# Seven block products in place of eight in the down projections of four convolution stages

## The chip, the cores and the metric

The kernel runs on one core of a Trainium2 chip. The metric is the device time of one execution in microseconds; of several runs the median is taken. TensorE is the engine that multiplies matrices (PE in the profile, with PEld for its weight loads), VectorE (DVE) does elementwise sums, ScalarE (ACT) the functions, GpSimd (POOL) and SyncE (SP) issue transfers.

## What is computed

The reference is a transformer in float32 with a sequence of 256 tokens and a width of 1024: two layers of a first kind, then four layers of a second kind. Each of the four ends with a gated feed-forward part with a short convolution:

```python
def conv_glu_ffn(h, up_w, conv_w, conv_b, down_w):
    gate, up = jnp.split(h @ up_w, 2, axis=-1)
    gate = causal_dwconv(gate, conv_w) + conv_b
    return (jax.nn.silu(gate) * up) @ down_w
...
        x = x + conv_glu_ffn(rmsnorm_2(x, ln_ffn[i]), f_up[i], f_conv_w[i], f_conv_b[i],
                             f_down[i]).astype(x.dtype)
```

The hidden width is 2816, which is 22 row blocks of 128. The change bears on the last product, the down projection: 256 tokens x 2816 times 2816 x 1024, added onto x. After the fourth layer a last RMS norm gives the output.

## The kernel before, in words

Everything is float32. The weights come as 244 chunks of 128 x 4096 (2 MB each) through `ring`, a buffer of four chunks: `chunk_load` on SyncE (line 2665) loads chunk c when TensorE has counted `chunks_used` up to c - 3, that is when chunk c - 4 has been used; `arrived` is an engine's wait for a chunk. The chunks are used strictly in order.

A convolution stage (`convglu_pe`, `convglu_act`, `convglu_dve`) goes through eleven chunks of the up projection. For chunk j TensorE computes 256 gate channels into one PSUM bank and 256 up channels into the next (banks 4 and 5 for even j, 6 and 7 for odd j; `channels_pe`, line 468). ScalarE copies the gate bank to `cbuf` (line 2343), VectorE does three taps of the convolution into `aT` (lines 2356 and 2362), ScalarE the SiLU (line 2347), and VectorE multiplies with the up bank (line 2367). That makes two of the 22 row blocks of `aT`, which is channels x tokens. VectorE counts `convglu_dve_done` four times a chunk, ScalarE `convglu_act_done` twice a chunk.

The down projection (`down_pe` with nk=22; in the last stage `last_pe`) takes six chunks with four row blocks each. For chunks 0 to 3 (16 row blocks; line 341, in the last stage line 1083) TensorE does, for each row block, two token tiles x two halves of the 1024 columns, into banks 0 to 3, bank 2t + half. A matmul is 128 x 128 weights against 128 x 512 moving data and becomes two TensorE instructions. The tail, chunks 4 and 5 with six row blocks (line 360, in the last stage 1095), is done first for token tile 0 and then for tile 1. Ahead of chunk 5 TensorE waits that the last up chunk's product is in `aT` (the `then` wait). When tile 0 is complete, VectorE adds banks 0 and 1 onto `x[:, 0]` (line 445; last stage 1114), ScalarE squares (line 402), VectorE takes the reciprocal and scales (453, 456), and TensorE transposes the scaled tile (line 390) between the chunks 4 and 5 of tile 1. Tile 1 follows in the same way, into the next stage. In the last stage the norm goes to the output instead (lines 1114, 1117, 1120, and the store 1131).

The order on each engine is written out by hand, and each engine's queue runs in that order: on VectorE `convglu_dve` is followed by `down_dve` (or `last_dve`). The four stages that the diff touches are those whose down projections are numbered 8, 11 and 14, and the last one; the other `down_pe` calls with nk=22 (after SwiGLU stages) are left as they are.

Of the kernel before, what the change touches and what calls it, by code (L numbers as in the profile page):

```python
# [6 lines left out]
P = 128  # L7
SEQ = 256
TT = SEQ // P
D = 1024  # L10
# [44 lines left out]
def build(nc, x_in, mem_in, weights_in, ada_in, b_gate_in, w_small1_in, w_small2_in, col_in, row_in, final_norm_in, rope_in, out):  # L55
    with ExitStack() as ctx:
# [4 lines left out]
        def sem(name):  # L61
            return ctx.enter_context(nc.semaphore(name))
# [63 lines left out]
        convglu_dve_done = sem("convglu_dve_done")  # L126
        hgrn_act_done = sem("hgrn_act_done")
# [196 lines left out]
        def down_pe(pe, i, before, c0, nk, ada=(), kc0=None, ki=0, late=None, then=None):  # L324
# [10 lines left out]
            for j in range(nc - 2):  # L335

                w = arrived(pe, c0 + j).rearrange("p (k c) -> p k c", k=4)
                for k in range(4):
                    for t in range(TT):
                        for half in range(2):  # L340
                            last = pe.matmul(ps[:, 2 * t + half, :], aT[:, 4 * j + k, t * P:(t + 1) * P],  # L341
                                             w[:, k, half * 512:(half + 1) * 512], start=(4 * j + k == 0), stop=False)
                last.then_inc(chunks_used, 1)
                if j < len(ada):
                    ada_reduce_pe(pe, ada[j], 6 + ada[j] % 2)
                if late and j == 0:
                    turn(pe, n, 3)
# [4 lines left out]
            for t in range(TT):  # L352
                for c in range(nc - 2, nc):
                    if then and (t, c) == (0, nc - 1):
                        pe.wait_ge(*then)
                    w = arrived(pe, c0 + c) if t == 0 else ring[:, (c0 + c) % R, :]
                    w = w.rearrange("p (k c) -> p k c", k=4)
                    for k in range(min(4, nk - 4 * c)):
                        for half in range(2):
                            last = pe.matmul(ps[:, 2 * t + half, :], aT[:, 4 * c + k, t * P:(t + 1) * P],  # L360
                                             w[:, k, half * 512:(half + 1) * 512], start=(4 * c + k == 0), stop=(4 * c + k == nk - 1))
                    if t == 1:
                        last.then_inc(chunks_used, 1)
# [56 lines left out]
        def down_dve(dve, i, before, c0, nk, gain, shift, gate=None, gi=0, ada=(), mg_col=None):  # L420
# [13 lines left out]
            if ada:  # L434
                ada_take_dve(dve, ada[-1], 6 + ada[-1] % 2)
                dve.wait_ge(ada_taken, ada[-1] + 1)

# [670 lines left out]
        def last_dve(dve):  # L1108

            dve.wait_ge(last_norm_loaded, 16)  # L1110
# [1257 lines left out]

        def hgrn_part(start, half):

            return view(big, start + 1024 * half, 4, SEQ)
# [346 lines left out]
        def _(pe):  # L2718
# [18 lines left out]
            down_pe(pe, 8, (convglu_dve_done, 40), c0=121, nk=22, then=(convglu_dve_done, 44))  # L2737
# [6 lines left out]
            down_pe(pe, 11, (convglu_dve_done, 84), c0=156, nk=22, then=(convglu_dve_done, 88))  # L2744
# [5 lines left out]
            down_pe(pe, 14, (convglu_dve_done, 128), c0=197, nk=22, then=(convglu_dve_done, 132))  # L2750
# [5 lines left out]
            last_pe(pe, (convglu_dve_done, 172), c0=238, then=(convglu_dve_done, 176))  # L2756
# [42 lines left out]
        def _(dve):  # L2799
# [18 lines left out]
            down_dve(dve, 8, (convglu_dve_done, 44), c0=121, nk=22, gain=column('ln_mix_2', 8, KT), shift=zeros)  # L2818
# [5 lines left out]
            down_dve(dve, 11, (convglu_dve_done, 88), c0=156, nk=22, gain=column('ln_mix_2', 16, KT), shift=zeros)  # L2824
# [5 lines left out]
            down_dve(dve, 14, (convglu_dve_done, 132), c0=197, nk=22, gain=column('ln_mix_2', 24, KT), shift=zeros)  # L2830
# [5 lines left out]
            last_dve(dve)  # L2836
# [109 lines left out]
```

## Time and profile before

| | us |
|---|---|
| median of three runs | 3842.44 (3839.93 to 3847.46) |
| profiled execution, whole | 3835.18 |
| its span, first to last instruction | 3833.5 |
| PE busy in the span | 3769.7 (98%) |
| DVE busy | 1064.5 (28%) |
| ACT busy | 722.6 (19%) |
| mean granted TensorE clock | 0.993 of full speed |

The profile is that of one execution. In its rows a PE matmul instruction has a duration of its own, but instructions are pipelined: the spacing from start to start is what adds up, and it is read from the busy time of an unbroken group divided by its count. "Idle before" is an engine's idle time ahead of an instruction, with what ended it. The chain that ended last is followed back from the last instruction, so its pieces are the work and waits that set the end.

### The profile page before, as it was taken

To read this page: it belongs to the slowest core of one execution; us is meant where nothing else is said; L and a number is where in the kernel's file an instruction comes from. 1 tells how busy PE (TensorE), PEld (TensorE's weight loads), DVE (VectorE), ACT (ScalarE), POOL (GpSimd) and SP (SyncE) were. 2 spreads that over 40 slices of the span, in tenths; PEclk is the share of its full clock that TensorE was granted. 3 is DMA by queue.
4 is the path that set the end of the run, shared out by engine and by line. 5 is a ranking of instruction groups with operands and counts; after the bars stand their busy time and mean duration, and the time that the engine had idled before them with its cause. 6 is when DMAs were issued, how large, how long until landed. Compare 5 with 4: busy or idle time off the path is not lost.

```text
span 3833.5 us, 37694 instructions
## 1 busy us (share of the span) xinstructions
PE 3769.7 (98%) x16628; PEld 2706.8 (71%) x16628; DVE 1064.5 (28%) x2082; ACT 722.6 (19%) x1370; POOL 16.2 (0%) x43
## 2 busy tenths in 40 slices
PE   6999999999999999999999999999999999999999
PEld 5856686784678587578766668677666967757784
DVE  5434342410520044102122112136411212431121
ACT  1003300100520053111011211033211103421110
POOL 1000000000000000000000000000000000000000
PEclk8999999999999999999999999999999999999999
DMA  9753486643334433334442434433233344333342
GB/s 376 287 192 133 175 307 230 248 159 148 132 123 154 154 132 110 132 132 154 153 154 88 152 114 154 154 132 110 89 133 129 142 151 149 110 132 132 140 151 99
DMA packets 42450, 598.43 MB, mean 156 GB/s; under 512 B 4736, under 2 KB 4752, under 8 KB 6192
## 3 DMA queue, kind: packets, MB, share of 16 engines
q1 hardware_dynamic: 41024, 589.94, 41.6%
q0 software_dynamic: 1264, 6.10, 0.4%
q8 instruction: 131, 2.15, 0.2%
q14 instruction: 31, 0.25, 0.0%
HBM read 594.97 MB, written 1.05 MB: 155 GB/s over the span
## 4 chain that ended last, share of the span: by engine, by line
PE 95%; DVE 3%; issue 1%; ACT 1%; DMA 0%; DVEq 0%
PE ps L468 37%; PE ps L341 12%; PE ps L360 9%; PE ps L1927 4%; PE ps L380 3%; PE ps L2268 3%; PE ps L1960 3%; PE ps L1435 2%; PE ps L1455 2%; PE ps L664 1%; PE ps L2486 1%; PE ps L1430 1%; PE ps L493 1%; PE ps L1083 1%; PE ps L390 1%
## 5 line engine op out<-in xcount | busy, mean ns | idle before, releaser
L468 PE MATMUL ps<-hT,ring 128*128 128x256 f32 (+1 forms) x7872 | 1438.3, 345 | 3.6 <-DVE stat L322 3.6
L468 PEld LDWEIGHTS ps<-hT,ring 128*128 128x128 f32 x7872 | 1291.8, 191 | 147.3 <-issue 7.7
L341 PE MATMUL ps<-ring,aT 128*128 128x512 f32 x1088 | 471.6, 594 | 0.0
L341 PEld LDWEIGHTS ps<-ring,aT 128*128 128x128 f32 x1088 | 206.7, 191 | 254.5 <-issue 254.1
L360 PE MATMUL ps<-ring,aT 128*128 128x512 f32 x784 | 341.1, 592 | 0.0
L360 PEld LDWEIGHTS ps<-ring,aT 128*128 128x128 f32 x784 | 147.9, 190 | 179.1 <-issue 178.9
L221 DVE SCALAR_TENSOR_TENSOR memT<-big,silu_c,memT 128x512 f32<-128x512 f32 x238 | 179.0, 752 | 8.5
L1927 PE MATMUL ps<-hT,ring 128*128 128x256 f32 x768 | 173.6, 382 | 0.0
L402 ACT ACTIVATE big<-x 128x1024 f32<-128x1024 f32 x34 | 35.9, 1057 | 729.6 <-DVE x L445 409.2
L1927 PEld LDWEIGHTS ps<-hT,ring 128*128 128x128 f32 x768 | 145.7, 192 | 26.2 <-issue 7.7
L2356 DVE TENSOR_SCALAR aT<-cbuf,col 128x256 f32<-128x256 f32 x88 | 27.1, 351 | 415.6 <-ACT cbuf L2343 415.6
L1180 DVE TENSOR_TENSOR aT<-cbuf,ps 128x512 f32<-128x512 f32 x44 | 30.2, 687 | 397.7 <-ACT cbuf L1164 397.7
L1164 ACT ACTIVATE cbuf<-ps 128x512 f32<-128x512 f32 x44 | 26.3, 597 | 578.5 <-PE ps L468 578.5
L445 DVE TENSOR_TENSOR x<-x,ps 128x1024 f32<-128x1024 f32 x22 | 26.9, 1221 | 357.6 <-PE ps L360 349.8
L1960 PE MATMUL ps<-ring,hT 128*128 128x512 f32 x256 | 113.4, 594 | 0.0
L2268 PE MATMUL ps<-ring,big 128*128 128x512 f32 x256 | 112.5, 592 | 0.0
L380 PE MATMUL ps<-big,ring 128*128 128x256 f32 x512 | 111.8, 379 | 0.0
L2089 DVE SCALAR_TENSOR_TENSOR big<-cbuf,col,big 128x256 f32<-128x256 f32 x192 | 80.3, 480 | 105.0 <-ACT big L1976 103.9
L380 PEld LDWEIGHTS ps<-big,ring 128*128 128x128 f32 x512 | 97.0, 190 | 14.7 <-issue 1.9
L2343 ACT COPY cbuf<-ps 128x512 f32<-128x512 f32 x44 | 25.7, 585 | 416.7 <-PE ps L468 416.7
L664 PE MATMUL ps<-hT,ring 128*128 128x256 f32 x448 | 101.3, 385 | 0.0
L664 PEld LDWEIGHTS ps<-hT,ring 128*128 128x128 f32 x448 | 85.4, 193 | 13.2 <-issue 1.9
(474 smaller groups left out, 3211.3 us busy)
## 6 DMA issues: line engine op xcount, KB each, us to landing
ring<-weights_in SPq DMA_DIRECT2D x244, 2048.0 KB, 7.7
big<-ada_in SPq DMA_DIRECT2D x34, 2048.0 KB, 7.7
ring<-ada_in SPq DMA_DIRECT2D x2, 2048.0 KB, 27.3
big<-b_gate_in POOLq DMA_DIRECT2D x1, 1536.0 KB, 15.1
x<-x_in SPq DMA_DIRECT2D x1, 1024.0 KB, 4.9
big<-b_gate_in POOLq DMA_DIRECT2D x1, 1024.0 KB, 9.3
big<-mem_in POOLq DMA_DIRECT2D x1, 1024.0 KB, 5.1
out<-big SPq DMA_DIRECT2D x2, 512.0 KB, 2.6
```

The costliest lines, as they stand in the source:

```text
L221: dve.scalar_tensor_tensor(out=ada_sum[:, a % 2, :], in0=w[:, k, :], scalar=silu_c[:, k:k + 1], in1=ada_sum[:, a % 2, :], op0=ALU.mult, op ...
L341: last = pe.matmul(ps[:, 2 * t + half, :], aT[:, 4 * j + k, t * P:(t + 1) * P], w[:, k, half * 512:(half + 1) * 512], start=(4 * j + k == ...
L360: last = pe.matmul(ps[:, 2 * t + half, :], aT[:, 4 * c + k, t * P:(t + 1) * P], w[:, k, half * 512:(half + 1) * 512], start=(4 * c + k == ...
L380: last = pe.matmul(ps[:, 4 + 2 * j + m // 2, (m % 2) * SEQ:(m % 2 + 1) * SEQ], w[:, k, m * P:(m + 1) * P], view(big, 0, KT, SEQ)[:, k, :], ...
L468: last = pe.matmul(ps[:, bank + m // 2, (m % 2) * SEQ + at:(m % 2) * SEQ + at + n], w[:, k, m * P:(m + 1) * P], hT[:, k, at:at + n], start ...
L664: last = pe.matmul(ps[:, bank + m // 2, (m % 2) * SEQ:(m % 2 + 1) * SEQ], w[:, k, m * P:(m + 1) * P], hT[:, k, :], start=(k == 0), stop=(k ...
L1435: last = pe.matmul(ps[:, bank, :], hT[:, k, half * P:(half + 1) * P], w[:, k, :], start=(k == 0), stop=(k == KT - 1))
L1455: last = pe.matmul(ps[:, 2 * t + half, :], aT[:, 4 * c + k, t * P:(t + 1) * P], w[:, k, half * 512:(half + 1) * 512], start=(c == 0 and k ...
L1927: last = pe.matmul(ps[:, bank + m // 2, (m % 2) * SEQ:(m % 2 + 1) * SEQ], w[:, k, m * P:(m + 1) * P], hT[:, k, :], start=(k == 0), stop=(k ...
L1960: last = pe.matmul(ps[:, 4 + 2 * (j % 2) + t, :], hT[:, k, t * P:(t + 1) * P], w[:, k, :], start=(k == 0), stop=(k == KT - 1))
L2089: last = dve.scalar_tensor_tensor(out=mamba_conv(j)[:, m, :], in0=cbuf[:, j % 2, m, 1 + tap:1 + tap + SEQ], scalar=col[:, w:w + 1], in1=ma ...
L2268: last = pe.matmul(ps[:, 4 + 2 * j + t, :], view(big, 0, KT, SEQ)[:, k, t * P:(t + 1) * P], w[:, k, :], start=(k == 0), stop=(k == KT - 1))
```

## The change

In chunks 0 to 3 of the four down projections the sixteen row blocks are taken as eight pairs. For a pair, the two token tiles of the two row blocks are the four blocks of a left matrix (a11 and a12 are tile 0 of the even and the odd row block, a21 and a22 tile 1 of them), and the two halves of the two rows of weights are the four blocks of a right matrix (b11, b12 the halves of the even row, b21, b22 of the odd). The 2 x 2 block product is done with seven block products and sums of the operands ahead and of the results behind (Winograd's form of Strassen's scheme):

- Left sums on VectorE, `seven_left_dve`, four instructions of 128 x 256 elements after the up chunks 1, 3, 5 and 7: s1 = a21 + a22, s2 = s1 - a11, a21 := a11 - a21 in place, s4 = a12 - s2. The three new ones lie in `big`.
- Right sums on VectorE, `seven_right_dve`, four instructions of 128 x 1024 elements for each down chunk: t1 = b12 - b11, t2 = b22 - t1, b12 := b22 - b12 in place in the ring, t4 = b21 - t2. They lie in `big` in two buffers by the chunk's parity. Those of down chunks 0 and 1 stand in `convglu_dve` after the products of up chunks 9 and 10, those of 2 and 3 at the head of `down_dve` or `last_dve`; the latter two first wait until TensorE is through with down chunk 0 or 1.
- TensorE, `seven_pe`: for each chunk seven products over its two pairs, into banks 0, 1, 4, 6, 7, 2 and 5 in this order, accumulated over all four chunks. It waits for the left sums ahead of the second product, for right sums ahead of the fourth, fifth and sixth; for chunk 0 also, ahead of the third, that ScalarE has copied bank 4 of up chunk 10 (`taken`), and ahead of the seventh, that VectorE has read bank 5 of it (`then`, which so moves from the tail to here).
- Result sums on VectorE, `seven_add_dve`, seven instructions when TensorE is through with down chunk 3: banks 4, 6, 7 and 5 are summed and added onto x. Banks 0, 1 and 2 hold the first parts of output blocks, on which the tail goes on accumulating; bank 3 is started by the tail. The tail itself, chunks 4 and 5, stays at eight products for two row blocks.

```diff
@@ new helpers, ahead of down_pe
+        def seven_left_part(i):
+
+            return view(big, 3072 + 1024 * i, 8, P)
+
+        def seven_right_part(j, i):
+
+            return view(big, 6144 + 3072 * (j % 2) + 1024 * i, 2, 512)
+
+        def seven_left_dve(dve, n, g, done, count):
+
+            q = slice(2 * g, 2 * g + 2)
+            rows = aT[:, 0:16, :].rearrange("p (q e) c -> p q e c", e=2)
+            a11, a12, a21, a22 = rows[:, q, 0, 0:P], rows[:, q, 1, 0:P], rows[:, q, 0, P:SEQ], rows[:, q, 1, P:SEQ]
+            s1, s2, s4 = (seven_left_part(i)[:, q, :] for i in range(3))
+            at = 16 * n + 4 * g
+
+            dve.wait_ge(done, count)
+            dve.tensor_tensor(s1, a21, a22, ALU.add).then_inc(seven_left, 1)
+            dve.wait_ge(seven_left, at + 1)
+            dve.tensor_tensor(s2, s1, a11, ALU.subtract).then_inc(seven_left, 1)
+            dve.tensor_tensor(a21, a11, a21, ALU.subtract).then_inc(seven_left, 1)
+            dve.wait_ge(seven_left, at + 2)
+            dve.tensor_tensor(s4, a12, s2, ALU.subtract).then_inc(seven_left, 1)
+
+        def seven_right_dve(dve, n, c0, j):
+
+            w = arrived(dve, c0 + j).rearrange("p (q e c) -> p q e c", q=2, e=2)
+            b11, b12, b21, b22 = w[:, :, 0, 0:512], w[:, :, 0, 512:D], w[:, :, 1, 0:512], w[:, :, 1, 512:D]
+            t1, t2, t4 = (seven_right_part(j, i) for i in range(3))
+            at = 16 * n + 4 * j
+
+            if j >= 2:
+                dve.wait_ge(chunks_used, c0 + j - 1)
+            dve.tensor_tensor(t1, b12, b11, ALU.subtract).then_inc(seven_right, 1)
+            dve.wait_ge(seven_right, at + 1)
+            dve.tensor_tensor(t2, b22, t1, ALU.subtract).then_inc(seven_right, 1)
+            dve.tensor_tensor(b12, b22, b12, ALU.subtract).then_inc(seven_right, 1)
+            dve.wait_ge(seven_right, at + 2)
+            dve.tensor_tensor(t4, b21, t2, ALU.subtract).then_inc(seven_right, 1)
+
+        def seven_pe(pe, n, c0, j, taken, freed):
+
+            at = 16 * n + 4 * j
+            w = arrived(pe, c0 + j).rearrange("p (q e c) -> p q e c", q=2, e=2)
+            t1, t2, t4 = (seven_right_part(j, i) for i in range(3))
+            s1, s2, s4 = (seven_left_part(i) for i in range(3))
+
+            def product(bank, left, right):
+                for q in range(2):
+                    last = pe.matmul(ps[:, bank, :], left(2 * j + q), right[:, q, :], start=(j == 0 and q == 0), stop=(j == 3 and q == 1), skip_group_check=True)
+                return last
+
+            product(0, lambda q: aT[:, 2 * q + 1, 0:P], w[:, :, 1, 0:512])
+            pe.wait_ge(seven_left, at + 4)
+            product(1, lambda q: s4[:, q, :], w[:, :, 1, 512:D])
+            if j == 0:
+                pe.wait_ge(*taken)
+            product(4, lambda q: aT[:, 2 * q, 0:P], w[:, :, 0, 0:512])
+            pe.wait_ge(seven_right, at + 2)
+            product(6, lambda q: s2[:, q, :], t2)
+            pe.wait_ge(seven_right, at + 3)
+            product(7, lambda q: aT[:, 2 * q, P:SEQ], w[:, :, 0, 512:D])
+            pe.wait_ge(seven_right, at + 4)
+            product(2, lambda q: aT[:, 2 * q + 1, P:SEQ], t4)
+            if j == 0:
+                pe.wait_ge(*freed)
+            product(5, lambda q: s1[:, q, :], t1).then_inc(chunks_used, 1)
+
+        def seven_add_dve(dve, n, c0):
+
+            part, both = gdn_work[:, 0:512], gdn_work[:, 512:D]
+            at = 7 * n
+
+            dve.wait_ge(chunks_used, c0 + 4)
+            dve.tensor_tensor(x[:, 0, 0:512], x[:, 0, 0:512], ps[:, 4, :], ALU.add).then_inc(seven_added, 1)
+            dve.tensor_copy(part, ps[:, 4, :]).then_inc(seven_added, 1)
+            dve.wait_ge(seven_added, at + 2)
+            dve.tensor_tensor(part, part, ps[:, 6, :], ALU.add).then_inc(seven_added, 1)
+            dve.wait_ge(seven_added, at + 3)
+            dve.tensor_tensor(x[:, 0, 512:D], x[:, 0, 512:D], part, ALU.add).then_inc(seven_added, 1)
+            dve.tensor_tensor(both, part, ps[:, 7, :], ALU.add).then_inc(seven_added, 1)
+            dve.wait_ge(seven_added, at + 5)
+            half = x[:, 1, :].rearrange("p (h c) -> p h c", h=2)
+            dve.tensor_tensor(half, half, both.unsqueeze(1).to_broadcast([P, 2, 512]), ALU.add).then_inc(seven_added, 1)
+            dve.wait_ge(seven_added, at + 6)
+            dve.tensor_tensor(x[:, :, 512:D], x[:, :, 512:D], ps[:, 5, :].unsqueeze(1).to_broadcast([P, TT, 512]), ALU.add).then_inc(seven_added, 1)
+
+        def down_pe(pe, i, before, c0, nk, ada=(), kc0=None, ki=0, late=None, then=None, seven=None, taken=None):
...
+                if seven is not None:
+                    seven_pe(pe, seven, c0, j, taken, then)
+                    continue
...
-                    if then and (t, c) == (0, nc - 1):
+                    if then and seven is None and (t, c) == (0, nc - 1):
...
+                            first = 4 * c + k == 0 if seven is None else (t, half, c, k) == (1, 1, nc - 2, 0)
                             last = pe.matmul(ps[:, 2 * t + half, :], aT[:, 4 * c + k, t * P:(t + 1) * P],
-                                             w[:, k, half * 512:(half + 1) * 512], start=(4 * c + k == 0), stop=(4 * c + k == nk - 1))
+                                             w[:, k, half * 512:(half + 1) * 512], start=first, stop=(4 * c + k == nk - 1), skip_group_check=seven is not None)
...
+            if seven is not None:
+                seven_right_dve(dve, seven, c0, 2)
+                seven_right_dve(dve, seven, c0, 3)
+                seven_add_dve(dve, seven, c0)
+                dve.wait_ge(seven_added, 7 * seven + 7)
...
@@ the last stage: last_pe and last_dve
-        def last_pe(pe, before, c0, then):
+        def last_pe(pe, before, c0, then, seven, taken):
...
-                w = arrived(pe, c0 + j).rearrange("p (k c) -> p k c", k=4)
-                for k in range(4):
-                    for t in range(TT):
-                        for half in range(2):
-                            last = pe.matmul(ps[:, 2 * t + half, :], aT[:, 4 * j + k, t * P:(t + 1) * P],
-                                             w[:, k, half * 512:(half + 1) * 512], start=(4 * j + k == 0), stop=False)
-                last.then_inc(chunks_used, 1)
+                seven_pe(pe, seven, c0, j, taken, then)
...
-                    if (t, c) == (0, 5):
-                        pe.wait_ge(*then)
...
-                                             w[:, k, half * 512:(half + 1) * 512], start=False, stop=(4 * c + k == 21))
+                                             w[:, k, half * 512:(half + 1) * 512], start=(t, half, c, k) == (1, 1, 4, 0), stop=(4 * c + k == 21), skip_group_check=True)
...
+        def last_dve(dve, c0, seven):
+
+            seven_right_dve(dve, seven, c0, 2)
+            seven_right_dve(dve, seven, c0, 3)
+            seven_add_dve(dve, seven, c0)
+            dve.wait_ge(seven_added, 7 * seven + 7)
...
@@ at the end of the loop over j in convglu_dve
+                if j % 2 and j < 8:
+                    seven_left_dve(dve, n, j // 2, convglu_dve_done, 44 * n + 4 * j + 4)
+                if j >= 9:
+                    seven_right_dve(dve, n, c0 + 11, j - 9)
...
@@ the four calls, one of them shown for each queue
-            down_pe(pe, 8, (convglu_dve_done, 40), c0=121, nk=22, then=(convglu_dve_done, 44))
+            down_pe(pe, 8, (convglu_dve_done, 40), c0=121, nk=22, then=(convglu_dve_done, 44), seven=0, taken=(convglu_act_done, 21))
-            down_dve(dve, 8, (convglu_dve_done, 44), c0=121, nk=22, gain=column('ln_mix_2', 8, KT), shift=zeros)
+            down_dve(dve, 8, (convglu_dve_done, 44), c0=121, nk=22, gain=column('ln_mix_2', 8, KT), shift=zeros, seven=0)
```

## Rows read from the trace of the kernel before

**Rows 1.** Page, parts 1 and 4: engines' busy time, and the chain by engine and line.
```profile
PE 3769.7 (98%) x16628; PEld 2706.8 (71%) x16628; DVE 1064.5 (28%) x2082; ACT 722.6 (19%) x1370; POOL 16.2 (0%) x43
...
PE 95%; DVE 3%; issue 1%; ACT 1%; DMA 0%; DVEq 0%
```

**Rows 2.** Chain in order of time: start us, us, what; three of the four stages.
```profile
1896.38 54.93 PE ps L341 x128
...
3118.68 54.93 PE ps L341 x128
...
3604.85 145.76 PE ps L468 x768
3750.61 54.93 PE ps L1083 x128
3805.54 20.61 PE ps L1095 x48
3826.16 0.02 issue
3826.18 1.23 DVE x L1114
```

**Rows 3.** Timeline (start us, us, engine, line), weight loads in down chunk 0.
```profile
3751.74 0.19 PEld L1083 LDWEIGHTS ps<-ring,aT 128*128 128x128 f32 x1 [0.24 <-issue]
3752.17 0.19 PEld L1083 LDWEIGHTS ps<-ring,aT 128*128 128x128 f32 x1 [0.24 <-issue]
3752.59 0.19 PEld L1083 LDWEIGHTS ps<-ring,aT 128*128 128x128 f32 x1 [0.24 <-issue]
```

**Rows 4.** The same across the border of down chunks 0 and 1.
```profile
3763.32 0.19 PEld L1083 LDWEIGHTS ps<-ring,aT 128*128 128x128 f32 x1 [0.24 <-issue]
3763.75 0.19 PEld L1083 LDWEIGHTS ps<-ring,aT 128*128 128x128 f32 x1 [0.24 <-issue]
3764.18 0.19 PEld L1083 LDWEIGHTS ps<-ring,aT 128*128 128x128 f32 x1 [0.24 <-issue]
3764.38 0.33 SPq L2665 DMA_DIRECT2D ring<-weights_in  x1
```

**Rows 5.** L341 alone: duration ns least/median/most, first and last start.
```profile
L341 PE MATMUL ps<-ring,aT x1088: 592/592/1061, 210.1 to 3440.4; 128*128 128x512 f32 x182
```

**Rows 6.** Groups by form, VectorE: line, op, form, count, busy us, mean ns.
```profile
L2123 DVE TENSOR_TENSOR big<-big 128x1024 f32<-128x1024 f32 x8 | 9.8, 1223 | 26.6 <-ACT big L2002 26.6
L2117 DVE TENSOR_TENSOR big<-big,gdn_work 128x256 f32<-128x256 f32 x16 | 6.8, 425 | 0.5
L2367 DVE TENSOR_TENSOR aT<-aT,ps 128x512 f32<-128x512 f32 x44 | 30.3, 688 | 42.9 <-ACT aT L2347 42.9
L445 DVE TENSOR_TENSOR x<-x,ps 128x1024 f32<-128x1024 f32 x22 | 26.9, 1221 | 357.6 <-PE ps L360 349.8 <-PE ps L1455 7.8
```

**Rows 7.** Timeline, VectorE, up chunks 9 and 10 of the last stage, and its tail.
```profile
3737.45 0.62 DVE L2356 TENSOR_SCALAR aT<-cbuf,col 128x256 f32<-128x256 f32 x2 [9.70 <-ACT cbuf L2343]
...
3740.88 0.69 DVE L2367 TENSOR_TENSOR aT<-aT,ps 128x512 f32<-128x512 f32 x1 [0.97 <-ACT aT L2347]
3751.27 0.62 DVE L2356 TENSOR_SCALAR aT<-cbuf,col 128x256 f32<-128x256 f32 x2 [9.70 <-ACT cbuf L2343]
3751.92 1.80 DVE L2362 SCALAR_TENSOR_TENSOR aT<-cbuf,col,aT 128x256 f32<-128x256 f32 x4
3754.69 0.69 DVE L2367 TENSOR_TENSOR aT<-aT,ps 128x512 f32<-128x512 f32 x1 [0.97 <-ACT aT L2347]
3815.95 1.22 DVE L1114 TENSOR_TENSOR x<-x,ps 128x1024 f32<-128x1024 f32 x1 [60.57 <-PE ps L1095]
```

**Rows 8.** Timeline, ScalarE, the copy of up chunk 10's gate bank.
```profile
3750.65 0.58 ACT L2343 COPY cbuf<-ps 128x512 f32<-128x512 f32 x1 [9.80 <-PE ps L468]
```

**Rows 9.** Timeline, VectorE and TensorE, the tail of down projection 11.
```profile
2506.95 0.75 DVE L456 TENSOR_SCALAR big<-x,stat 128x1024 f32<-128x1024 f32 x1
...
2492.20 17.33 PE L360 MATMUL ps<-ring,aT 128*128 128x512 f32 x40
2509.37 1.04 PE L390 MATMUL ps<-ident,big 128*128 128x128 f32 x8
```

**Rows 10.** Page, part 6: issue, KB each, median us to landing.
```profile
ring<-weights_in SPq DMA_DIRECT2D x244, 2048.0 KB, 7.7
```

**Rows 11.** Around 2779 us: window (us, busy PE PEld DVE ACT POOL, clock, DMA), PE timeline.
```profile
2778.00:2782.00 4.00, 4.00 (x12) 2.18 (x13) 3.08 (x6) 1.92 (x10) 0.00 (x0) 0.61 0.00 0
...
2778.30 0.73 PE L731 MATMUL ps<-ident,big 128*128 128x128 f32 x5
2778.85 4.01 PE L341 MATMUL ps<-ring,aT 128*128 128x512 f32 x5
```

More of the change, by code:

```diff
@@ L126, in build @@
         convglu_dve_done = sem("convglu_dve_done")
+        seven_left, seven_right, seven_added = sem("seven_left"), sem("seven_right"), sem("seven_added")
         hgrn_act_done = sem("hgrn_act_done")
@@ L322, in norm_dve @@
             dve.memset(stat[:, 63:64], 0.0).then_inc(norm_dve_done, 1)
-        def down_pe(pe, i, before, c0, nk, ada=(), kc0=None, ki=0, late=None, then=None):
+        def seven_left_part(i):
[15 more added lines that the diff above has]
+            dve.tensor_tensor(s4, a12, s2, ALU.subtract).then_inc(seven_left, 1)
@@ L418, in down_act, with down_dve @@
                 act.copy(view(big, 2048, KT, SEQ)[:, 4:8, :], ps[:, 6:8, :].rearrange("p b (m c) -> p (b m) c", m=2)).then_inc(down_k_done, 1)
-        def down_dve(dve, i, before, c0, nk, gain, shift, gate=None, gi=0, ada=(), mg_col=None):
+        def down_dve(dve, i, before, c0, nk, gain, shift, gate=None, gi=0, ada=(), mg_col=None, seven=None):
             nc = -(-nk // 4)
@@ L1106, in last_act @@
                 act.activation(stat[:, t:t + 1], stat[:, t:t + 1], ACT.Sqrt, bias=stat[:, 62:63]).then_inc(last_act_done, 1)
-        def last_dve(dve):
+        def last_dve(dve, c0, seven):
[3 more added lines that the diff above has]
+            dve.wait_ge(seven_added, 7 * seven + 7)
             dve.wait_ge(last_norm_loaded, 16)
@@ L2743, in _ @@
             convglu_pe(pe, 1, 10, c0=145, w_col=COL['f_conv_w_2'] + 66, b_col=COL['f_conv_b_2'] + 22)
-            down_pe(pe, 11, (convglu_dve_done, 84), c0=156, nk=22, then=(convglu_dve_done, 88))
+            down_pe(pe, 11, (convglu_dve_done, 84), c0=156, nk=22, then=(convglu_dve_done, 88), seven=1, taken=(convglu_act_done, 43))
             gdn_pe(pe, 11, c0=162)
@@ L2749, in _ @@
             convglu_pe(pe, 2, 13, c0=186, w_col=COL['f_conv_w_2'] + 132, b_col=COL['f_conv_b_2'] + 44)
-            down_pe(pe, 14, (convglu_dve_done, 128), c0=197, nk=22, then=(convglu_dve_done, 132))
+            down_pe(pe, 14, (convglu_dve_done, 128), c0=197, nk=22, then=(convglu_dve_done, 132), seven=2, taken=(convglu_act_done, 65))
             mamba_pe(pe, 1, 14, c0=203)
@@ L2755, in _ @@
             convglu_pe(pe, 3, 16, c0=227, w_col=COL['f_conv_w_2'] + 198, b_col=COL['f_conv_b_2'] + 66)
-            last_pe(pe, (convglu_dve_done, 172), c0=238, then=(convglu_dve_done, 176))
+            last_pe(pe, (convglu_dve_done, 172), c0=238, then=(convglu_dve_done, 176), seven=3, taken=(convglu_act_done, 87))
         @block.scalar
@@ L2823, in _ @@
             convglu_dve(dve, 1, c0=145, w_col=COL['f_conv_w_2'] + 66, b_col=COL['f_conv_b_2'] + 22)
-            down_dve(dve, 11, (convglu_dve_done, 88), c0=156, nk=22, gain=column('ln_mix_2', 16, KT), shift=zeros)
+            down_dve(dve, 11, (convglu_dve_done, 88), c0=156, nk=22, gain=column('ln_mix_2', 16, KT), shift=zeros, seven=1)
             gdn_dve(dve, w_col=COL['g_conv_w_2'])
@@ L2829, in _ @@
             convglu_dve(dve, 2, c0=186, w_col=COL['f_conv_w_2'] + 132, b_col=COL['f_conv_b_2'] + 44)
-            down_dve(dve, 14, (convglu_dve_done, 132), c0=197, nk=22, gain=column('ln_mix_2', 24, KT), shift=zeros)
+            down_dve(dve, 14, (convglu_dve_done, 132), c0=197, nk=22, gain=column('ln_mix_2', 24, KT), shift=zeros, seven=2)
             mamba_dve(dve, 1, w_col=COL['m_conv_w_2'] + 128, nw_col=COL['m_norm_w_2'] + 16)
@@ L2835, in _ @@
             convglu_dve(dve, 3, c0=227, w_col=COL['f_conv_w_2'] + 198, b_col=COL['f_conv_b_2'] + 66)
-            last_dve(dve)
+            last_dve(dve, c0=238, seven=3)
 def _columns(a):
```

## The prediction

> **What bounds the kernel now.** I read the page's engine times first: TensorE is busy for 98% of the span, VectorE for 28%, ScalarE for 19%, and the chain that ended last is 95% TensorE, with no share of DMA [rows 1]. So work taken off TensorE shortens the kernel, if nothing in the same stage becomes late. Then the chain in order of time, for the four stages that change. In each the sixteen row blocks are one unbroken piece of 128 TensorE instructions in 54.93 us; three of the four pieces stand in [rows 2], and the fourth, at 2437.43 us, has the same length. The pieces ahead of it (up chunks) and behind it (the tail) are unbroken too [rows 2]. The spacing of instructions is 54.93 / 128 = 0.429 us. The duration of one is longer, 0.592 us [rows 5], since they overlap; only the spacing adds up. Last I read the timeline of VectorE and ScalarE in the last stage: after up chunk 10 VectorE works until 3754.69 + 0.69 = 3755.38 us, and then stands idle for 60.57 us, until tile 0 of the tail is complete [rows 7]. That hole is where most of the new sums go.
>
> **TensorE's part.** Per down chunk the change does seven products over two pairs, 14 matmuls, where there were 4 row blocks x 2 tiles x 2 halves = 16. A matmul of this shape is two instructions (64 matmuls make the 128 of [rows 2]). So 4 chunks x 2 matmuls x 2 = 16 instructions go per stage, each of 0.429 us: 6.87 us a stage, 27.5 us in four. The piece becomes 112 x 0.429 = 48.1 us. The tail keeps its 48 instructions in 20.61 us [rows 2].
>
> Will the 112 keep the spacing? Every instruction already loads weights of its own; a load takes 0.19 us and stands idle for 0.24 us before the next [rows 3], so other weights in each product cost nothing. The moving side is 512 contiguous columns as before. VectorE's work beside it does not stretch it: at 3751.92 to 3753.72 us VectorE is busy [rows 7], and the loads come at 3751.74, 3752.17, 3752.59, the same 0.43 us apart [rows 3].
>
> **The added waits.** Per chunk seven_pe has four new waits, and chunk 0 two more, one of which is only moved from the tail: 17 more per stage, 68 in all. What a wait costs that is already fulfilled shows at the border of chunks 0 and 1: the chunk's arrival is waited for with the load at 3763.75, and the loads stay 0.43 us apart on both sides [rows 4]. I take 0. The other end: if every one broke the overlap of two instructions, it would cost 0.592 - 0.429 = 0.163 us [rows 2, 5], in all 68 x 0.163 = 11.1 us. Below zero there is nothing, a wait gives no time back.
>
> **Are the waits fulfilled?** Let 0 be the end of up chunk 10 (3750.61 us in the last stage), when TensorE begins the down projection.
> - Bank 4 (`taken`): ScalarE's copy ends at 3750.65 + 0.58 = 3751.23, at 0.6 us [rows 8]. TensorE asks for it after two products, 8 x 0.429 = 3.4 us.
> - Bank 5 (`then`): the product of up chunk 10 is in `aT` at 4.8 us (3755.38). It is asked for ahead of the seventh product, 24 x 0.429 = 10.3 us.
> - Right sums of down chunk 0: VectorE begins them after up chunk 9's product, at 3740.88 + 0.69 = 3741.57, that is -9.0 us. Four instructions of 1024 elements from SBUF cost 1.223 us each [rows 6]: 4.9 us. They end near -4.1 us, ahead of up chunk 10's taps at 0.7 us, so that those aren't late. Their data: the chunk is issued when up chunk 7 is used, over 27 us before, and lands 7.7 us after its issue [rows 10].
> - Right sums of chunk 1: from 4.8 to 9.7 us, wanted at 12.0 + 5.1 = 17.2 us. Chunks 2 and 3: VectorE waits for the buffer until TensorE has left chunk 0 or 1 (12.0, 24.0 us), is done at 16.9 and 28.9 us, and the first is wanted at 29.2 and 41.2 us. Queued behind these waits on VectorE are only the result sums, which start at 48.1 us. Chunk 3 itself, issued at 0, lands at 7.7 us; chunk 4 is issued at 12.0 and wanted at 48.1.
> - Left sums: four of 256 elements at 0.425 us [rows 6], 1.7 us after up chunks 1, 3, 5 and 7. VectorE has about 9.7 us idle per up chunk [rows 7]; wanted far later.
> - Result sums: five of 512 elements at 0.688 us (the copy too, by the nearest row) and two of 1024 at 1.221 us [rows 6] give 5.9 us, some 6.3 with a small gap at each dependence. They run beside tile 0 of the tail, 24 x 0.429 = 10.3 us, so VectorE is free 4.0 us before it must add tile 0. Behind that stands a second reserve: in down projection 11 the scaled tile is ready at 2507.70, and TensorE transposes it, its matmuls unbroken, at 2509.37 [rows 9], 1.7 us.
>
> All cost 0 on the path. They add 16 x 0.425 + 16 x 1.223 + 5.9 = 32.3 us of VectorE a stage, 129 us in all, and cover for it is there in the hole above. Doubled, the result sums would take 11.8 us, 1.5 us too long for tile 0 and still inside the second reserve in that stage.
>
> The transfers keep their count. Down chunks are used every 12.0 instead of 13.7 us, against 7.7 us from issue to landing [rows 10]; so no chunk is late next.
>
> **The clock.** The granted clock is 1.00 in these stretches but isn't everywhere: at 2778 to 2782 us it is 0.61 on average, partly the level of 1.2 GHz, after broken transpose work, and five matmul instructions take 4.01 us there: less the last one's 0.59 us [rows 5], four spacings of 0.854 us instead of 0.429 [rows 11]. The stages that change have no such break in [rows 2], and I add none. This drop costs 4 x (0.854 - 0.429) = 1.7 us. As the later stages move by 7 us and more, such a drop may come or go; I allow two each way, 3.4 us.
>
> **The sum.** Profiled execution: 3835.18 - 27.5 = 3807.7 us, its span 3833.5 - 27.5 = 3806.0. The median of the runs is 7.3 us above the profiled one. On the median: 3842.4 - 27.5 = 3814.9 us, -0.71%.
>
> **Rivals.**
> 1. Each added wait breaks the pipeline once. For it: there are 68, up to three within one chunk's middle. Against it: [rows 4]. Time: 3814.9 + 11.1 = 3826.0 us.
> 2. TensorE slows down to the lower clock level in the product pieces, because seven banks in turn and a wait before nearly each product make short breaks. For it: [rows 11], where the pieces ahead were broken up and the next ran at half rate. Against it: the product pieces have nothing to wait for by the list above, and in the kernel before the banks already change after every two instructions (bank 2t + half) in pieces that keep 0.429 us [rows 2]. Price: 0.854 - 0.429 = 0.425 us per instruction [rows 11]; it takes away the whole gain from 27.5 / 0.425 = 65 of the 448 instructions on. If all 448 ran so: 3814.9 + 448 x 0.425 = 4005 us, slower by 4%. The Trainium skill, "TensorE: Matmul & The Clock Gate", section "A second HAM failure mode: psum-queue depth-cycling", tells of it as a rule: a kernel that cycled through PSUM banks idled for short moments between groups of matmuls and fell back to the lower rate again and again. By that rule the time would be this rival's; the trace of before, where the banks change and the rate stays, does not agree with it for this shape of work.
> 3. VectorE's sums become the bound. For it: TensorE waits for some of them in every chunk. It needs sums much longer than the 1.22 us of [rows 6]. With 3.5 us each the sixteen right sums and the 4.1 us of up chunk 10's work between them run from -9.0 us to -9.0 + 16 x 3.5 + 4.1 = 51.1 us, and the last two products follow, 3.4 us: the piece ends at 54.5 us instead of 48.1, and 6.4 of a stage's 6.9 us are gone: 3840.5 us. Against it: no sum of two float32 operands of 1024 elements in [rows 6] is above 1.23 us, and it would need a factor of 2.9.
> 4. The change doesn't remove the instructions (fewer matmuls but the same time, by another split): 3842 us. Speaking against: the two instructions per matmul come with type and shape, which stay.
>
> **How the numbers follow.** Forecast 0.85, rival 1 0.06, rival 2 0.04, rival 3 0.03, rival 4 0.02. What a measurement can tell from no change is about 0.2%, 7.7 us. Faster: forecast and rival 1, 0.91. Same: rivals 3 and 4, 0.05. Slower: rival 2, 0.04. Range: below, 3814.9 - 3.4 (clock) less some 4.5 for the spread of runs (those shown lie 2.5 below to 5 above their median) = 3807; above, rival 1's end, 3826.0, which also takes in the clock and the spread, 3.4 + 5. The time is the forecast's.
>
> **What would show it.** Right: pieces of 112 instructions in 48.1 us, four times, with no TensorE idle before; VectorE near 1194 us busy; PE near 3742 us. Wrong: idle time on TensorE ended by VectorE's sums (3); the same pieces at 59 us and more, or a clock below 1.00 in them (2); single gaps of some 0.16 us at each product (1). The same VectorE add (line 445) starting later than the end of tile 0 would mean that result sums are too long.

## The result and the profile after

The changed kernel took 3820.2 us (median of 5 runs, 3813.1 to 3823.3), against 3843.9 us for the kernel before in the same session: ratio 0.9935, with a 95% interval of 0.9921 to 0.9950. Two more sessions gave 0.9908 (0.9896 to 0.9921) and 0.9923 (0.9904 to 0.9942). The forecast was 3814.9 us, a ratio of 0.9928. It is faster, by 0.65 to 0.92% in the three sessions, and the range 3807 to 3826 held the time.

The first lines of the page after, to be read against [rows 1]:

```profile
span 3815.5 us, 37729 instructions
## 1 busy us (share of the span) xinstructions
PE 3751.4 (98%) x16564; PEld 2703.3 (71%) x16564; DVE 1186.5 (31%) x2238; ACT 723.1 (19%) x1370; POOL 16.4 (0%) x43
```

TensorE runs 64 instructions fewer (16628 to 16564), as the four stages should give, and VectorE 156 more. But PE's busy time fell by 18.3 us and the span by 18.0, not by 27.5. The chain in order of time, the four pieces of seven products and the end (compare [rows 2]):

```profile
1896.18 48.07 PE ps L374 x112
...
2430.36 48.07 PE ps L374 x112
...
3114.45 48.07 PE ps L374 x112
...
3593.76 145.76 PE ps L566 x768
3739.52 48.07 PE ps L374 x112
3787.59 20.61 PE ps L1185 x48
3808.20 0.02 issue
3808.23 1.23 DVE x L1208
```

Each piece went from 54.93 us for 128 to 48.07 us for 112: 6.86 us, four times, 27.4 us. The spacing is the same 0.429 us. So the stages that were changed gave all that was expected of them, and 9.4 us went elsewhere in this execution. Where shows in windows from the end of the piece of down projection 11 to the first matmul of down projection 12, before and after; columns as in the first line of [rows 11]. This middle stage is the tail of down projection 11 and the gated delta net behind it. TensorE's instructions in it are those of before; VectorE has the result sums more.

```profile
2492.36:2779.03 286.67, 273.27 (x1594) 206.19 (x1593) 145.72 (x298) 92.39 (x191) 1.11 (x2) 0.99 0.30 111
```
```profile
2478.43:2774.83 296.40, 283.02 (x1594) 215.24 (x1593) 151.43 (x306) 92.48 (x191) 1.11 (x2) 0.95 0.29 107
```

The same 1594 matmul instructions took 9.7 us longer, and the mean granted clock was 0.95 in place of 0.99. That is the missing part. One group of this stage in the two chains, again before and after:

```profile
2740.75 2.79 PE ps L706 x26
```
```profile
2729.59 5.40 PE ps L804 x26
```

The granted clock is 1.00 in the first and 0.50, the level of 1.2 GHz, in the second. The mean clock of a whole span doesn't show this. It was 0.993 before and 0.995 after, because in the trace before the clock is also 0.50 from 20 to 47 us, where in the trace after it is 1.00. That costs almost nothing, since TensorE is busy for only 7.5 of those 27 us: the chain begins its second unbroken group of up-chunk matmuls at 64.18 us before and at 63.94 us after. Whether the change causes the slow groups is what the first experiments ask.

TensorE's timeline in the first chunk of the last stage after the change, each product a group of four instructions, and VectorE's beside it:

```profile
3739.36 1.88 PE L374 MATMUL ps<-ring,aT 128*128 128x512 f32 x4
3741.08 1.88 PE L374 MATMUL ps<-ring,big 128*128 128x512 f32 x4
3742.79 1.88 PE L374 MATMUL ps<-ring,aT 128*128 128x512 f32 x4
3744.51 1.88 PE L374 MATMUL ps<-big 128*128 128x512 f32 x4
3746.23 1.88 PE L374 MATMUL ps<-ring,aT 128*128 128x512 f32 x4
3747.94 1.88 PE L374 MATMUL ps<-big,aT 128*128 128x512 f32 x4
3749.66 1.88 PE L374 MATMUL ps<-big 128*128 128x512 f32 x4
```
```profile
3730.40 1.22 DVE L358 TENSOR_TENSOR big<-ring 128x1024 f32<-128x1024 f32 x1
3731.65 1.23 DVE L360 TENSOR_TENSOR big<-ring,big 128x1024 f32<-128x1024 f32 x1
3732.79 1.22 DVE L361 TENSOR_TENSOR ring<-ring 128x1024 f32<-128x1024 f32 x1
3733.93 1.22 DVE L363 TENSOR_TENSOR big<-ring,big 128x1024 f32<-128x1024 f32 x1
3740.18 0.62 DVE L2450 TENSOR_SCALAR aT<-cbuf,col 128x256 f32<-128x256 f32 x2 [5.03 <-ACT cbuf L2437]
...
3787.63 0.69 DVE L399 TENSOR_TENSOR x<-x,ps 128x512 f32<-128x512 f32 x1 [19.21 <-PE ps L374]
...
3792.26 1.22 DVE L410 TENSOR_TENSOR x<-x,ps 128x1024 f32<-128x1024 f32 x1
3798.03 1.22 DVE L1208 TENSOR_TENSOR x<-x,ps 128x1024 f32<-128x1024 f32 x1 [4.55 <-PE ps L1185]
```

The products follow one another every 1.72 us, four times 0.429, whatever bank and operand they have and whatever wait stands between them. The right sums of chunk 0 end at 3735.15 us, 4.4 us before TensorE begins the down projection and 5.03 us before VectorE is next needed. The result sums start 0.04 us after the piece, take 5.85 us and leave 4.55 us until tile 0.

### The profile page after: what moved, and what is told of

The parts are those of the page before. It is cut to its first block, busy times and chain, and to the rows that moved or that the text cites. A ratio compares the mean times of both kernels' runs of the same rounds, so it can differ in the third digit from the quotient of the medians.

```text
span 3815.5 us, 37729 instructions
## 1 busy us (share of the span) xinstructions
PE 3751.4 (98%) x16564; PEld 2703.3 (71%) x16564; DVE 1186.5 (31%) x2238; ACT 723.1 (19%) x1370; POOL 16.4 (0%) x43
## 4 chain that ended last, share of the span: by engine, by line
PE 95%; DVE 3%; issue 1%; ACT 1%; DMA 0%; DVEq 0%
PE ps L566 37%; PE ps L452 9%; PE ps L432 8%; PE ps L374 5%; PE ps L2021 4%; PE ps L472 3%; PE ps L2362 3%; PE ps L2054 3%; PE ps L1529 2%; PE ps L1549 2%; PE ps L762 2%; PE ps L2585 1%; PE ps L1524 1%; PE ps L591 1%; PE ps L482 1%
## 5 line engine op out<-in xcount | busy, mean ns | idle before, releaser
L452 PE MATMUL ps<-ring,aT 128*128 128x512 f32 x784 | 341.1, 592 | 0.0
L432 PE MATMUL ps<-ring,aT 128*128 128x512 f32 x704 | 306.3, 595 | 0.0
L452 PEld LDWEIGHTS ps<-ring,aT 128*128 128x128 f32 x784 | 147.9, 190 | 179.1 <-issue 178.9
L432 PEld LDWEIGHTS ps<-ring,aT 128*128 128x128 f32 x704 | 133.7, 191 | 163.9 <-issue 163.7
L2054 PE MATMUL ps<-ring,hT 128*128 128x512 f32 x256 | 113.4, 594 | 0.0
L1529 PE MATMUL ps<-ring,hT 128*128 128x512 f32 x192 | 90.7, 603 | 0.0
## 6 DMA issues: line engine op xcount, KB each, us to landing
ring<-ada_in SPq DMA_DIRECT2D x2, 2048.0 KB, 27.5
```

The costliest lines, as they stand in the source:

```text
L1529: last = pe.matmul(ps[:, bank, :], hT[:, k, half * P:(half + 1) * P], w[:, k, :], start=(k == 0), stop=(k == KT - 1))
L2054: last = pe.matmul(ps[:, 4 + 2 * (j % 2) + t, :], hT[:, k, t * P:(t + 1) * P], w[:, k, :], start=(k == 0), stop=(k == KT - 1))
```

## The experiments

Two theories stood against each other at first. The main one: the four pieces give 27.4 us, sums and waits nothing, and the rest of any difference is TensorE's lower clock level in stages the change doesn't touch, which comes and goes from execution to execution. The rival: sums and waits, or a longer middle stage, are a cost of the change. The expectations for a2 and b2 count the middle stage from 17.17 us later, behind the 40 instructions of the tail, so that 286.67 and 296.40 us are 269.5 and 279.2 there.

**Both kernels once more.** No edit.

> The changed kernel once more. Main theory: the four pieces of 112 instructions stay at 48.07 us each in every execution, and what varies from execution to execution is how long TensorE is at its lower clock level outside of them. Then the stage between down projection 11 and 12 (279.2 us in the first trace of the changed kernel, 269.5 us before, with the same instructions) comes out at another length here, most likely 268 to 275 us, and the time is 3815 to 3823 us. Rival, the change itself slows that stage: it stays at 279 us, 3820 us.

> The kernel before once more. Main theory: four pieces of 128 instructions of 54.93 us; the stage between down projections 11 and 12 varies with the lower clock level here too, between 267 and 280 us, 3840 to 3848 us in all. Rival, the change slows that stage: here it stays at 269.5 us (within 2 us).

The changed kernel took 3813.6 us (4 runs), the kernel before 3844.7 us (11 runs) as b2 and 3846.9 us (23 runs, 3832.2 to 3853.7) as the comparison. The middle stage, first in the changed kernel (a2), then in the kernel before (b2):

```profile
2475.12:2771.52 296.40, 283.00 (x1594) 215.21 (x1593) 151.41 (x305) 92.47 (x191) 1.11 (x2) 0.95 0.29 107
```
```profile
2489.67:2789.48 299.81, 285.73 (x1593) 217.16 (x1593) 146.42 (x299) 93.21 (x197) 1.11 (x2) 0.94 0.29 106
```

In a2 the stage was as long as in the first trace after, 296.4 us; that alone would have spoken for the rival, and the 268 to 275 us that I had called likely did not come. The time, 3813.6 us, lay just below its 3815 to 3823 as well. But the kernel before, without any part of the change, took 299.8 us for it in b2 (282.6 as the expectation counts it, above its 267 to 280) and 286.7 us in its first trace. The stage varies by 13 us in an unchanged kernel, more than what was missing, and the clock goes along with it (0.99 to 0.94).

Two traces of each kernel would be thin evidence, but a kernel further down settles it. The one with eight right sums a chunk contains the whole change and more, and in its trace the stage is as short as in the first trace before:

```profile
2479.18:2765.82 286.64, 273.24 (x1594) 206.19 (x1593) 151.40 (x305) 92.38 (x191) 1.10 (x2) 0.99 0.30 111
```

Its whole time was 3808.3 us, against the 3807.7 forecast for an execution like the first trace before. So the change does not by itself make the stage slow, and the missing 9.4 us were a difference between two executions. Whether it makes slow executions of this stage more frequent can't be told from so few traces: all three of the changed kernel itself had 296 to 299 us.

**Sums and waits without their gain.** An eighth product per pair, into a bank whose content the tail replaces:

```diff
-            product(5, lambda q: s1[:, q, :], t1).then_inc(chunks_used, 1)
+            product(5, lambda q: s1[:, q, :], t1)
+            product(3, lambda q: aT[:, 2 * q + 1, P:SEQ], w[:, :, 1, 512:D]).then_inc(chunks_used, 1)
```

> The changed kernel with an eighth product per pair into bank 3, whose content the tail's first matmul replaces: all sums and waits of the change, but as many TensorE instructions as before. Main theory (only the instruction count matters, sums and waits cost nothing): pieces of 128 instructions in 54.9 us, the time of the kernel before, 3843.9 us, ratio to it 1.000. Rival (the sums and waits cost the part of the forecast gain that is missing, some 4 to 9 us): 3848 to 3853 us.

3845.2 us (11 runs), ratio to the kernel before 0.9993 (0.9981 to 1.0005). The pieces:

```profile
1893.04 54.93 PE ps L374 x128
...
3750.05 54.93 PE ps L374 x128
```

With as many instructions as before, the time is that of before, although all 156 VectorE instructions and all waits are in it. At 54.93 us the piece is the same to the last digit, so a wait that is already fulfilled costs nothing that the trace can show. The interval excludes a cost above 2 us (0.0005 x 3844), in this one session.

**The gain without the sums.** All calls of seven_left_dve, seven_right_dve and seven_add_dve removed, and TensorE's waits for them:

```diff
-                if j % 2 and j < 8:
-                    seven_left_dve(dve, n, j // 2, convglu_dve_done, 44 * n + 4 * j + 4)
-                if j >= 9:
-                    seven_right_dve(dve, n, c0 + 11, j - 9)
...
-                seven_right_dve(dve, seven, c0, 2)
-                seven_right_dve(dve, seven, c0, 3)
-                seven_add_dve(dve, seven, c0)
...
-            pe.wait_ge(seven_left, at + 4)
...
-            pe.wait_ge(seven_right, at + 2)
...
```

> The changed kernel without any left, right or result sum on VectorE and without TensorE's waits for them: the seven products run on whatever the operands' buffers hold, and only banks 0 to 3 reach x. Main theory: 3816 to 3820 us, the same as the changed kernel, ratio to the kernel before 0.993. Rival (sums and waits cost the missing part): 3811 to 3815 us, that is the full 27.5 us or more below the kernel before.

Its output is not that of the reference, since the operands are left as they lie; it only measures time. 3816.3 us (6 runs, 3804.8 to 3822.9), ratio 0.9915 (0.9901 to 0.9930), pieces again 48.07 us. That is 30.6 us below the kernel before, which taken alone would fit the rival too (27.5 us or more). But the changed kernel, with all its sums, was 33.3 us below it in the same session (ratio 0.9908): leaving the sums out gained nothing. Its middle stage was longer than any of the five above, with no sum in the kernel:

```profile
2478.22:2780.32 302.10, 288.76 (x1593) 219.91 (x1593) 146.34 (x299) 93.21 (x197) 1.11 (x2) 0.93 0.29 105
```

Together the two kernels settle it: the time that the change takes off is that of the 64 instructions, and the sums and waits cost nothing that shows in the pieces or, to within 2 us, in the times of the kernel with the eighth product.

**How much cover the right sums have.** The changed kernel hides them; these two kernels look for the point where it no longer would, by doing the last sum of a chunk five or nine times, each after the one before:

```diff
-            dve.tensor_tensor(t4, b21, t2, ALU.subtract).then_inc(seven_right, 1)
+            for again in range(9):
+                if again:
+                    dve.wait_ge(seven_right, at + 3 + again)
+                dve.tensor_tensor(t4, b21, t2, ALU.subtract).then_inc(seven_right, 1)
```

> The changed kernel with the last right sum (t4) of each chunk done five times, each after the one before: eight sums of 1024 elements a chunk in place of four, some 9.8 us in place of 4.8 (spacing 1.14 to 1.25 us each in the trace of the changed kernel). Main theory (the right sums have a reserve of about 12.0 us a chunk): pieces of 112 instructions stay at 48.1 us, the time at that of the changed kernel, 3807 to 3823 us. Rival (TensorE is already held close to the sums, so that doubling them shows): pieces of 52 us and more.

> The same with t4 nine times: twelve sums a chunk, some 14.8 us, more than the 12.0 us of TensorE's work in a chunk. Main theory (the sum chain sets the end of the piece once it is longer): sums from -9.0 us, four chunks of 14.8 us and 4.1 us of the last up chunk's work end at 54.3 us, two products of 3.4 us follow: the piece with its waits takes 57.7 us in place of 48.1, 9.6 us more, 38 us in four stages, so about 3850 to 3862 us. Rival (there are further reserves): pieces below 53 us.

With eight sums a chunk the four pieces stay at 48.07 us, and the time was 3808.3 us. With twelve it was 3845.9 us (one run each; the kernel before beside them 3846.2), 4 us below the 3850 to 3862 expected. The difference of the two kernels, 37.6 us, is near the 38 us expected; it is the starting point of the sum that was too high for these executions. TensorE's timeline in the last stage of the twelve-sum kernel, its start, the three waits, and its end, and VectorE's over two chunks of it:

```profile
3757.99 1.88 PE L377 MATMUL ps<-ring,aT 128*128 128x512 f32 x4
...
3782.67 2.81 PE L377 MATMUL ps<-big,aT 128*128 128x512 f32 x4 [3.92 <-DVE big L366]
3785.27 2.80 PE L377 MATMUL ps<-big 128*128 128x512 f32 x4
3787.91 1.88 PE L377 MATMUL ps<-ring,aT 128*128 128x512 f32 x4
...
3797.42 1.98 PE L377 MATMUL ps<-big,aT 128*128 128x512 f32 x4 [0.77 <-DVE big L366]
...
3812.16 1.98 PE L377 MATMUL ps<-big,aT 128*128 128x512 f32 x4 [2.46 <-DVE big L366]
3813.99 1.88 PE L377 MATMUL ps<-big 128*128 128x512 f32 x4
3815.70 14.76 PE L1188 MATMUL ps<-ring,aT 128*128 128x512 f32 x34
```
```profile
3782.54 1.22 DVE L358 TENSOR_TENSOR big<-ring 128x1024 f32<-128x1024 f32 x1
...
3786.07 11.30 DVE L366 TENSOR_TENSOR big<-ring,big 128x1024 f32<-128x1024 f32 x9
3797.28 1.22 DVE L358 TENSOR_TENSOR big<-ring 128x1024 f32<-128x1024 f32 x1
```

From 3757.99 to 3815.70 it is 57.7 us, where the sum chain of the forecast gave 57.7. TensorE waits 3.92 + 0.77 + 2.46 = 7.2 us, and most of the rest of the 9.6 us is this: the two groups of four behind the pause of 3.92 us take 5.24 us from start to start (3782.67 to 3787.91) in place of 8 x 0.429 = 3.43, at a mean granted clock of 0.67.

These 1.8 us of slower matmuls are not a cost on top of the chain. VectorE's sums follow one another without a gap, chunk after chunk every 14.74 us, and set the end of the piece. The slow groups only use up part of the next wait, which is 0.77 us, while the one after it, with no slow group ahead, is 2.46. The other three stages show the same: waits of 3.92, 0.76 or 0.77 and 2.45 or 2.46 us, and 5.24 us for the two groups behind the first. Behind a wait that no later sum takes up, such slow groups would count in full, as in the next kernel.

**How much cover the result sums have.** Two sums of 4096 elements ahead of them:

```diff
             dve.wait_ge(chunks_used, c0 + 4)
+            dve.tensor_tensor(held, parts, parts, ALU.add).then_inc(seven_added, 1)
+            dve.wait_ge(seven_added, at - 1)
+            dve.tensor_tensor(held, parts, parts, ALU.add).then_inc(seven_added, 1)
```

> The changed kernel with two extra sums of 4096 elements (about 4.4 us each, result not used) ahead of the result sums: VectorE then is free 4.4 us after tile 0 of the tail is complete. Main theory (first reserve 4.5 us, second reserve 1.6 us between the scaled tile and the transposes): TensorE waits about 2.8 us ahead of the transposes in the three inner stages, nothing in the last one, 8.4 us in all. Rival (the result sums have no reserve beyond the first): 4.4 us in each of four stages, 17.6 us.

The waits of TensorE in this kernel (us in total, times, longest) have one new line:

```profile
PE ps L486 <- DVE big L558: 7.8, 3, 2.6
```

2.6 us in each of the three inner stages and none in the last one, as the two reserves give it (7.8 us in all, 8.4 expected). One of the three cost more than its wait; in the chain of that stage the eight matmul instructions behind the transposes take 5.13 us, against 3.44 in the kernel before at the same place and in the other two stages:

```profile
1963.35 1.09 PE ps L486 x8
1964.44 5.13 PE ps L456 x8
```

The time, 3832.3 us, is a single run and tells less than these lines: in its trace the middle stage took 304.3 us, 17.6 more than in the first trace before, and only 2.6 of that is the added wait.

**The scheme in two more stages.** Down projections 3 and 5 (after SwiGLU) have no modulation weights to be summed beside them. Their left sums were put after up chunk 7, the right sums as in the convolution stages, and the result sums multiply by the gate:

```diff
+                if n >= 2 and j == 7:
+                    for g in range(4):
+                        seven_left_dve(dve, n - 2, g, swiglu_dve_done, 11 * n + j + 1)
+                if n >= 2 and j >= 9:
+                    seven_right_dve(dve, n - 2, c0 + 11, j - 9)
...
+            step(part, part, ps[:, 6, :], ALU.add)
+            step(both, part, ps[:, 7, :], ALU.add)
+            step(part, part, hi, ALU.mult, wait=False)
+            step(wide, both.unsqueeze(1).to_broadcast([P, 2, 512]), gate.rearrange("p (h c) -> p h c", h=2), ALU.mult)
+            step(x[:, 0, 512:D], x[:, 0, 512:D], part, ALU.add, wait=False)
+            step(both, ps[:, 5, :], hi, ALU.mult)
+            step(half, half, wide, ALU.add, wait=False)
+            step(part, ps[:, 4, :], lo, ALU.mult, wait=False)
+            step(x[:, :, 512:D], x[:, :, 512:D], both.unsqueeze(1).to_broadcast([P, TT, 512]), ALU.add)
+            step(x[:, 0, 0:512], x[:, 0, 0:512], part, ALU.add)
```

> The changed kernel with the same scheme in down projections 3 and 5 too (the two SwiGLU stages without modulation weights to sum in them; their result is multiplied by a gate, so that the result sums are eleven instructions, about 9.8 us, beside 10.3 us of the tail). Main theory: two more pieces go from 128 to 112 instructions, 54.93 to 48.07 us, 13.7 us less than the changed kernel: ratio to the kernel before 0.989, 3801 to 3806 us. Rival (the longer result sums are late for tile 0): the pieces shrink, but TensorE waits ahead of the transposes, and 5 us or less is gained over the changed kernel.

3802.8 us (6 runs, 3793.5 to 3808.5), ratio to the kernel before 0.9889 (0.9871 to 0.9908), against an expected 0.989. The two new pieces in its chain, and VectorE in the first of these stages, from the last matmul of the piece to tile 0:

```profile
860.19 48.07 PE ps L374 x112
1254.87 48.07 PE ps L374 x112
```
```profile
908.30 0.69 DVE L411 COPY gdn_work<-ps 128x512 f32<-128x512 f32 x1 [19.21 <-PE ps L374]
...
915.39 1.95 DVE L407 TENSOR_TENSOR x<-x,gdn_work 128x1024 f32<-128x1024 f32 x2
918.67 1.22 DVE L580 TENSOR_TENSOR big<-ps,big 128x1024 f32<-128x1024 f32 x1 [1.33 <-PE ps L483]
```

The eleven result sums take 9.04 us, and 1.33 us of the first reserve are left. This version is faster than the kernel before. The changed kernel did not run beside it; that it gains 13.7 us over it rests on the two pieces, since the ratios of separate sessions overlap (0.9871 to 0.9908 here, 0.9896 to 0.9921 for a2).

**The ratio once more.** No edit.

> The changed kernel a third time, for its ratio to the kernel before: 0.9935 [0.9921, 0.9950] and 0.9908 [0.9896, 0.9921] so far. Main theory (the change takes 27.5 us, and the rest of a difference between medians is how the lower clock level falls outside of the pieces in the few executions timed): a ratio near 0.9928, between 0.9912 and 0.9945, pieces of 48.07 us. Rival (the change brings a loss of its own of some 4 to 9 us outside of its pieces): 0.9938 or above.

3813.3 us (6 runs) against 3843.6 us (11 runs): 0.9923 (0.9904 to 0.9942), pieces of 48.07 us. The three ratios of the changed kernel, 0.9935, 0.9908 and 0.9923, lie on both sides of 0.9928, which is the 27.4 us. As times they are 23.7, 33.3 and 30.3 us, 29 on average, so a loss of 4 us or more of the change's own isn't supported. But the second interval (0.9896 to 0.9921) excludes 0.9928 and only touches the first: the times of a session give the gain to some 5 us at best, and its exact size is known from the pieces.

## Why the prediction held, point by point

- **TensorE's part**: 16 instructions a stage at 0.429 us, 6.87 us; measured 6.86 us, in all four stages, in every trace of the changed kernel. This is the mechanism of the forecast, and it held.
- **The added waits**: taken at 0, with 0.163 us each as the other end; measured 0 (pieces of 54.93 us with the eighth product). Rival 1 falls.
- **The order of events**: right sums of chunk 0 forecast from -9.0 to -4.1 us; in the last stage they ran from -9.1 to -4.4 us. The result sums took 5.85 us, forecast 6.3. The two reserves behind them (4.0 and 1.7 us in the forecast) measured 4.55 us and, from the added 8.9 us (two sums of 4.42) and the wait of 2.6 us, about 1.7 us (8.9 - 4.55 - 2.6).
- **VectorE's busy time** was forecast at 1194 us and is 1186.5: sums that don't depend on the one before start 1.14 us apart instead of 1.22, and 0.34 instead of 0.42 us for the short ones.
- **Rival 3** (sums as the bound) was priced as a chain; the kernel with twelve sums bore out this kind of sum (57.7 us). At the change's four sums it isn't near.
- **Rival 2** (lower clock level in the pieces) did not happen: without pauses the seven banks in turn keep 0.429 us. That it can follow a pause was right (twelve sums, first wait, in all four stages). The section of the Trainium skill's page "TensorE: Matmul & The Clock Gate" that was named there speaks of short idle moments between groups; the pieces have none, and so don't test it.
- **The clock outside of the pieces** is the term that was mis-sized. I allowed 3.4 us each way, twice the 1.7 us of one drop in one trace; the same trace had another, uncounted one (mean clock 0.95 from 2532.57 to 2600 us). The middle stage alone came out between 286.6 and 302.1 us in ten traces, with the same TensorE instructions. The kernel before ran between 3831.7 and 3853.7 us in the later sessions, where its first three runs had shown 3839.9 to 3847.5. The range held because it also took in the spread of runs: 3814.9 + 3.4 + 5 = 3823.3 us would have held the 3820.2 without rival 1's end at 3826, the 3.4 us alone would not. The medians of the three sessions, 3820.2, 3813.6 and 3813.3 us, lie 5.3 above to 1.6 below the forecast 3814.9. Its closeness has some luck in it: it starts from a median of three runs, 3842.4 us, and the kernel before had 3843.6 to 3846.9 in the sessions.
- **Profiled execution**: forecast 3807.7 us, measured 3817.6, for the same reason. PE's busy time was to be near 3742 us and is 3751.4, by the same 9.4 us.

## What to carry to other kernels

Where one engine is busy for 98% of the span and its pieces are unbroken, instructions taken from it count in full, provided that each sum that it then depends on has its start and its deadline written down; a forecast by spacing, not by duration, was right to 0.01 us a piece. Ask also how far the cover reaches: here the sums of a chunk could double, and with three times as many the gain was gone. And a difference of some microseconds between two traces has to be looked for in stages that the change doesn't touch before it is laid to the change.

## What the runs showed of the hardware

The middle stage has the same TensorE instructions in every kernel. In ten traces it took:

| trace | us | mean granted clock |
|---|---|---|
| eight right sums a chunk | 286.6 | 0.99 |
| before | 286.7 | 0.99 |
| twelve right sums a chunk | 288.2 | 0.98 |
| eighth product | 289.1 | 0.98 |
| two more stages | 292.3 | 0.96 |
| after | 296.4 | 0.95 |
| after again (a2) | 296.4 | 0.95 |
| after a third time (a3) | 298.8 | 0.94 |
| before again (b2) | 299.8 | 0.94 |
| without the sums | 302.1 | 0.93 |

The length follows the clock, whichever kernel it is. In the first trace after, the clock falls to the lower of its two levels, 1.2 GHz, behind a wait of 1.78 us followed by 128 matmuls of 32 x 32, and again behind a wait of 1.11 us, among matmuls of 64 x 64. In the first trace before, the same matmuls stand behind waits of 1.81 and 1.11 us, and the clock stays at 1.00. So the same work and waits are followed by the lower level in some executions and not in others. Why was not tried.

Pauses in otherwise dense work can have the same effect. Behind the 3.92 us of waiting the clock stayed at 1.00 for the first instructions and then fell; the next eight took 5.24 us in place of 3.43, in all four stages, so that by 1.81 / 0.425 some four of them were at the lower level (an estimate from the spacings at either level). Behind waits of 0.77 and 2.46 us in the same stage none was (1.98 and 1.88 us a group, clock 1.00), and behind one of three waits of 2.6 us the next eight took 5.13 us in place of 3.44.
